# Splitting the first weight loads of a fused transformer block into transfers of 32 partitions

## The chip, the cores and the metric

The kernel runs on one core of one Trainium2 chip. The metric is the device time of one execution in microseconds (us), as the median of several runs. A core has a matrix engine (PE; its weight loads are listed apart, as PEld), a vector engine (DVE), a scalar engine (ACT), a general engine (POOL) and a synchronising engine (SP), and 16 DMA engines that they share. In this kernel SP does nothing but issue transfers: it walks through a list written by hand, waits at each entry for a semaphore, and issues.

## The reference

One layer of a hybrid block over 256 tokens of width 1024, all in float32:

```python
u = rmsnorm(h, norm_mix[i])
proj = u @ w_in[i]
y_rw  = rwkv7_mix(token_shift(proj[..., :RW_COLS], shift_mu[i]), ...)   # 8 heads x 64
y_gla = gla_mix(proj[..., RW_COLS:], ...)                               # 4 heads, 64 / 128
h = h + jnp.concatenate([y_rw, y_gla], axis=-1) @ w_out[i]
u = rmsnorm(h, norm_ffn[i])
h = h + moe(u, ...)        # top 4 of 32 experts; per expert w1 1024 x 2048, w2 1024 x 1024
u = rmsnorm(h, norm_ple[i])
h = h + jax.nn.sigmoid(u @ w_ple_gate[i]) * (p[i] @ w_ple[i])
return rmsnorm(h, norm_final)
```

The weights of all 32 experts are read, whatever the router picks: 8.39 MB of w1 and 4.19 MB of w2 for each expert, some 403 MB in all.

## The kernel before

**Stages.** The mixer comes first: norm, input projection, the RWKV heads by chunks of 64 tokens, the GLA heads, the output projection with `w_out`. Then the router, then the experts one after the other, then the gate of the per-layer embedding and the last norm. With the largest expert's token count at 64 or below, as here, each expert is one pass over 64 token slots: gather the tokens by a matmul, the w1 stage (`w1_stage`, line 1854), clamp and activation, the w2 stage (`w2_stage`, line 1882), and a scatter by a matmul into sums that stay open in PSUM.

**Weight buffers.** Every expert weight chunk is 128 partitions of 4096 floats, 16 KB in a partition, 2.097 MB in all. A w1 is four chunks, a w2 is two. There are four w1 buffers for even experts (`W1B[0]`, in the tensor `ring`), four for odd experts (`W1B[1]`, laid over the mixer's tensors `lg`, `ka`, `bu`, `bkv`), and two w2 buffers that all experts share (`W2B`, in `ring`). So even experts' buffers and w2 buffers come free as the mixer is done with that part of the ring, odd experts' buffers as the mixer is done with those tensors.

**First fill.** SP's list (lines 353 to 383) issues `w_out` in two loads of 2.097 MB (`load_wout`), and then the first fill of the ten expert buffers, ten loads of 2.097 MB, each behind its own wait: w1 of expert 0 in the order 0, 1, 3, 2 of its chunks, w1 of expert 1 in the order 0, 3, 1, 2, and both chunks of expert 0's w2. Between them stand a second load of `x` (1.05 MB, line 365) and the load of `b1` (line 375), 32 rows of 8 KB into 32 partitions.

**Stream.** Then SP waits for the router's count (`cnt_ok`, line 414) and runs `stream` (line 385): for each expert it waits until PE has used a chunk (`w1_used`, `w2_used`) and issues the load of the chunk that follows in that buffer. After the last w2 it issues the 4.19 MB of `w_ple_gate` into the ring (line 421), which the tail needs. All these loads are on SP's one queue, which each DMA engine works off in order. ACT issues two loads on a queue of its own when the first tokens are gathered (lines 758 and 759: `p` 0.26 MB, `w_ple` 1.05 MB).

**PE's waits.** A transfer adds 16 to its semaphore when it is complete. PE waits for `b1` at line 1800, for `w_out` at lines 1722 and 1761. In the w1 stage it waits for chunk 1 first (`start=START`), and then for each chunk as it comes to it:

```python
pe.wait_ge(on[start], h * 16 + 16)
for k in range(KC):
    if k % 2 == 0:
        pe.wait_ge(on[k // 2], h * 16 + 16)
```

Of the kernel before, what the change touches and what calls it, by code (L numbers as in the profile page):

```python
# [25 lines left out]
P = 128  # L26
# [49 lines left out]
def hybrid_block(nc, x, p, norm_mix, w_in, shift_mu, rw_w0, rw_w2, rw_a0, rw_a2, rw_g2, rw_kk, rw_ka, rw_rk,  # L76
# [8 lines left out]
    with ExitStack() as ctx:  # L85
# [9 lines left out]
        def slot(i, n=1):  # L95
            return RING[:, i * SLOT_F:(i + n) * SLOT_F]
# [65 lines left out]
            return a.rearrange("p (h t) -> p h t", h=HP)  # L162

        HALF = (slice(0, 64), slice(64, 128))


        MT = slot(2, 2).rearrange("p (m w) -> p m w", m=16)
# [38 lines left out]
        W1B = ([slot(2 * c, 2) for c in range(W1C)], [LG[:, 0:4096], KA[:, :], BU[:, :], BKV[:, :]])  # L206
        W2B = [slot(8 + 2 * c, 2) for c in range(W2C)]
# [18 lines left out]
        def col(name, i, n=1):  # L226
# [3 lines left out]
        x_in, x1_in, vec_in, small_in, wout_in, wout2_in, rows_in, brow_in, out_done = (  # L230
            sem(s) for s in ("x_in", "x1_in", "vec_in", "small_in", "wout_in", "wout2_in", "rows_in", "brow_in", "out_done"))
        nm_in, lora_in = sem("nm_in"), sem("lora_in")
        win = [sem(f"win{i}") for i in range(7)]
        landed_e = [sem(f"landed_e{i}") for i in range(W1C)]
        landed_o = [sem(f"landed_o{i}") for i in range(W1C)]
        landed_2 = [sem(f"landed_2{i}") for i in range(W2C)]
# [62 lines left out]
        w1_v = w1.rearrange("a e (c q j) n -> a e c q (j n)", q=P, j=2)  # L299
        w2_v = w2.rearrange("a e (c q j) n -> a e c q (j n)", q=P, j=4)  # L300
# [5 lines left out]
        def _(sp):  # L306
# [3 lines left out]
            def load_cols(i, s, n, c0, w):  # L310
                dst = RING[:, s * SLOT_F:s * SLOT_F + KC * w].rearrange("p (k n) -> p k n", k=KC)
                sp.dma_start(dst, w_in[0, :, c0:c0 + w].rearrange("(k q) n -> q k n", q=P)).then_inc(win[i], 16)

            def load_w1(e, odd, c):
                sp.dma_start(W1B[odd][c], w1_v[0, e, c]).then_inc((landed_o if odd else landed_e)[c], 16)

            def load_w2(e, c):
                sp.dma_start(W2B[c], w2_v[0, e, c]).then_inc(landed_2[c], 16)  # L318

            load_cols(0, 0, 1, 3 * RW, 256)  # L320
            for name, k in VROWS[1:]:
                sp.dma_start(VEC[VAT[name]:VAT[name] + k, :], vec_src[name]).then_inc(vec_in, 16)
# [23 lines left out]

            def load_wout(first, s, signal):

                sp.dma_start(slot(s, 2).rearrange("p (k n) -> p k n", k=4),
                             w_out[0, first:first + 512, :].rearrange("(k q) n -> q k n", q=P)).then_inc(signal, 16)  # L350

            sp.wait_ge(tile_ps, 18)
            sp.dma_start(GLN, gla_norm[0].partition_broadcast(P)).then_inc(rows_in, 16)
# [4 lines left out]
            for r, src in enumerate((rw_gn_w, rw_gn_b)):  # L358
                sp.dma_start(GNWB[:, r, :], src[0].partition_broadcast(P)).then_inc(rows_in, 16)
            sp.wait_ge(gg_ps, 2)  # L360
            load_w1(0, 0, 0)
            sp.wait_ge(go_ps, 2)
            load_w2(0, 0)
            sp.wait_ge(wu_ps, 2)
            sp.dma_start(XB3, x.rearrange("a (t q) d -> q (a t) d", q=P)).then_inc(x_in, 16)
            sp.wait_ge(y_gla, 1)
            load_w1(1, 1, 0)
            sp.wait_ge(reff_ps, 1)
            load_w1(0, 0, 1)
            sp.wait_ge(bv_ok, 1)  # L370
            load_w1(1, 1, 3)
            sp.wait_ge(o_ps, 3)
            load_w2(0, 1)
            sp.wait_ge(ovar, 3)
            sp.dma_start(B1R[0:NE, :], b1[0]).then_inc(b1_in, 16)
            sp.wait_ge(wg_used, 1)
            load_w1(0, 0, 3)
            sp.wait_ge(yt_ps, 4)
            load_w1(1, 1, 1)
            sp.wait_ge(wout_used, 1)  # L380
            load_w1(0, 0, 2)
            sp.wait_ge(lg_ps, 3)
            load_w1(1, 1, 2)

            def stream(nb):

# [852 lines left out]
        def _(pe):  # L1239
# [110 lines left out]
            for grp in TOK_ORDER:  # L1350
# [12 lines left out]
                if grp == 7:  # L1363
                    for first in range(2):
                        for h in range(HP):
                            for c in range(2):
                                for q in range(2):
                                    j, tt = (q, q) if first == 0 else (1 - q, q)
                                    rj = HALF[j]
                                    ins = mm(bank(6 + tt)[rj, P * h + 64 * c:P * h + 64 * (c + 1)],  # L1370
# [23 lines left out]
            def mats(n, u):  # L1394
# [5 lines left out]
                if n >= 2:  # L1400
                    pe.wait_ge(mat_ok, n - 1)
                quarters = [(c, j, HALF[j], slice(P * t + 64 * c, P * t + 64 * (c + 1)), slice(64 * c, 64 * (c + 1)))
                            for c in range(2) for j in range(2)]
# [315 lines left out]
            pe.wait_ge(h_ok, 3)  # L1719
            read_out()  # L1720
            pe.wait_ge(yt_a, 2)
            pe.wait_ge(wout_in, 16)
            w_out_gla(0, (4,))
            pe.wait_ge(reff_ok, 2)
            pe.wait_ge(o_ps, 2)
# [32 lines left out]

            ms = RT8[3]
            pe.wait_ge(yt_a, 3)  # L1760
            pe.wait_ge(wout2_in, 16)
            w_out_rest(0, 0, range(4))
            turn_rwkv(1)
            w_out_rest(0, 1, range(4)).then_inc(wout_ps, 1)
# [89 lines left out]
            def w1_stage(i, h, odd, start=START, ple=None):  # L1854

                pe.wait_ge(xg_ok, i + 1)
                pe.wait_ge(t_ok, i * 2 + 1)

                on = landed_o if odd else landed_e
                pe.wait_ge(on[start], h * 16 + 16)  # L1860
                for k in range(KC):
                    if k % 2 == 0:
                        pe.wait_ge(on[k // 2], h * 16 + 16)
                    w = W1B[odd][k // 2][:, 2048 * (k % 2):2048 * (k % 2 + 1)]
                    for half in range(2):
                        if ple is not None and k == 0 and half == 1:
                            pe.wait_ge(pt_ok, 2 * ple + 2)
                        mm(bank(4 + half)[0:64, :], XG[:, k, :], w[:, 512 * half:512 * (half + 1)], k == 0, k == KC - 1, True)
                        ins = mm(bank(4 + half)[64:128, :], XG[:, k, :], w[:, FF + 512 * half:FF + 512 * (half + 1)], k == 0, k == KC - 1, True)
                        if k == KC - 1 and half == 0:  # L1870
                            ins.then_inc(h0_ps, 1)
                    if k % 2:
                        ins.then_inc(w1_used, 1)
# [8 lines left out]
            def w2_stage(i, h, odd, last=False, ple=None, held=0):  # L1882

                if last:
                    turn_back(i, 6)
                else:
                    pe.wait_ge(oh_ok, i + 2)
                    if held:
                        pe.wait_ge(pt_ok, held)
                    gather()  # L1890
                pe.wait_ge(hs0, i + 1)
                for c in range(KC):
                    if c == 4:
                        pe.wait_ge(hs1, i + 1)
                    ins = pe.transpose(bank(4 + c // 4)[:, P * (c % 4):P * (c % 4 + 1)], HS[:, P * c:P * (c + 1)], ID[:, :])  # L1895
                    if c % 4 == 3:
                        ins.then_inc(t_ps, 1)
                pe.wait_ge(ys_ok, i + 1)
                scatter(scattered)
                for k in range(KC):  # L1900
                    if k == 4 and not last:
                        pe.wait_ge(t_ok, i * 2 + 3)
                        turn_back(i, 4)
                        gather_turn(i + 1)
                        if ple == 0:
                            pe.wait_ge(ple_in, 32)
                            for n in range(2):
                                for t in range(TT):
                                    ins = pe.transpose(bank(5)[:, 256 * n + P * t:256 * n + P * (t + 1)], PX[:, t, P * n:P * (n + 1)], ID[:, :])
                            ins.then_inc(pt_ps, 1)  # L1910
                    if k % 4 == 0:
                        pe.wait_ge(act_ok, i * 2 + (k // 4 + 1))
                        pe.wait_ge(landed_2[k // 4], h * 32 + 16 * (odd + 1))
                    w = W2B[k // 4][:, 1024 * (k % 4):1024 * (k % 4 + 1)]
                    mm(bank(7)[0:64, :], ACTT[:, k, :], w[:, 0:512], k == 0, k == KC - 1, True)
                    ins = mm(bank(7)[64:128, :], ACTT[:, k, :], w[:, 512:1024], k == 0, k == KC - 1, True)
                    if k % 4 == 3:
                        ins.then_inc(w2_used, 1)
                pe.wait_ge(ohgt_ok, i + 2)
                if ple is not None:  # L1920
                    pe.wait_ge(pt_ok, 1)
                    ple_product(1, ple)
                    pe.wait_ge(xg_ok, i + 2)
                    ple_product(0, ple)
# [34 lines left out]
            def tail():  # L1959

                def raised(t):

                    for g in range(2):
                        pe.wait_ge(scaled, 4 + 2 * t + g)
                        turned(t, range(4 * g, 4 * g + 4), g if t else 4 + g)

                raised(0)
                pe.wait_ge(wout_in, 32)
                for n, (t, c, w, b) in enumerate(UNITS):
                    if n == 1:  # L1970
                        raised(1)
                    for k in range(KC):
                        if k % 4 == 0:
                            pe.wait_ge(ut_v, 12 + 2 * t + k // 4)
                        ins = mm(bank(b)[:, 0:w], UT3[:, k, P * t:P * (t + 1)], PLG[:, k, c:c + w], k == 0, k == KC - 1)
                    ins.then_inc(pg_ps, 1)
# [33 lines left out]
```

## Time and profile before

| | before |
|---|---|
| median of 3 runs | 1161.89 us (1159.8 to 1163.87) |
| the profiled execution, its own time | 1160.67 us |
| span of its trace, first to last instruction | 1159.0 us |
| PE busy | 1097.5 us, 95% of the span |
| PE weight loads busy | 492.2 us, 42% |
| DVE, ACT, POOL busy | 317.4, 217.5, 54.5 us |
| DMA, mean over the span | 373 GB/s, 432.21 MB |
| granted clock of PE, mean | 0.984 |
| chain that ended last, by engine | PE 56%, DMA 40% |

The span is 1.7 us shorter than the execution's time. Busy time of PE counts matmuls from start to modelled end, pipelined ones too, so 95% doesn't say that PE is the bound. The chain that ended last is followed back from the last instruction: a DMA in it is a transfer that something waited for, from its issue to its landing, so the time in which it stood in its queue is in it.

### The profile page before, as it was taken

Reading aid. Unit: us, or ns where it says so; the run is one execution under the profiler, and the core shown is the slowest. Engines: PE = TensorE matmul, PEld = TensorE weight load, DVE = VectorE, ACT = ScalarE, POOL = GpSimd, SP = SyncE. Lnnn points to the kernel's source line nnn. Section 1 sums busy time; section 2 is a strip of 40 time slices with the busy share of each in tenths; the row PEclk is TensorE's granted clock in tenths of the full one; section 3 lists DMA queues with packets and bytes.
Section 4 is the critical chain, followed back from the end, with each engine's and each line's share of the span. In section 5 each row is a group of like instructions: output and inputs, shape, how many; then the busy total and the mean of one; then the engine's idle time right before and its main releaser. Section 6 shows DMA issues by size and latency. Waiting matters only on the chain.

```text
span 1159.0 us, 16059 instructions
## 1 busy us (share of the span) xinstructions
PE 1097.5 (95%) x6367; PEld 492.2 (42%) x6368; DVE 317.4 (27%) x736; ACT 217.5 (19%) x397; POOL 54.5 (5%) x104
## 2 busy tenths in 40 slices
PE   8999889999999999999999999999999999999997
PEld 6876774433333333333333333333333333333334
DVE  3363454322222222222222222222222222222223
ACT  3233222211112111111111111112111111111124
POOL 8005220000000000000000000000000000000000
PEclk9999999899999999999999999999999999999999
DMA  9621178899999999999999999999999999999970
GB/s 335 206 82 52 52 286 343 357 427 426 431 428 429 429 428 429 428 429 428 428 429 429 428 429 428 430 427 429 430 429 428 429 428 428 429 428 428 428 317 38
DMA packets 42095, 432.21 MB, mean 373 GB/s; under 512 B 5364, under 2 KB 8808, under 8 KB 16936
## 3 DMA queue, kind: packets, MB, share of 16 engines
q1 hardware_dynamic: 41352, 430.10, 88.7%
q10 hardware_dynamic: 704, 1.58, 0.4%
q8 instruction: 26, 0.43, 0.2%
q14 instruction: 13, 0.11, 0.0%
HBM read 430.62 MB, written 1.05 MB: 372 GB/s over the span
## 4 chain that ended last, share of the span: by engine, by line
PE 56%; DMA 40%; issue 1%; POOL 1%; DVE 1%; ACT 1%; SPq 0%; DVEq 0%; POOLq 0%; ACTq 0%
PE ps L1241 52%; DMA ring<-in_w_dram 37%; DMA ring<-in_w_ple_gate_dram 2%; PE ps L1895 1%; PE ps L1822 1%; PE ps L1879 0%; DMA xb<-in_x_dram 0%; POOL xb L533 0%; PE ps L1743 0%; PE ps L1530 0%; ACT bu L662 0%; PE ps L1797 0%; SPq L318 0%; PE ps L1377 0%; POOL ring L518 0%
## 5 line engine op out<-in xcount | busy, mean ns | idle before, releaser
L1241 PE MATMUL ps<-ring,ay 128*64 128x512 f32 x1024 | 242.1, 616 | 37.2 <-DMA ring<-in_w_dram 36.2
L1241 PE MATMUL ps<-ring,gqk 128*64 128x512 f32 x1024 | 224.1, 595 | 2.8 <-DMA ring<-in_w_dram 2.6
L1156 DVE COPY t<-ps 128x512 f32<-128x512 f32 x32 | 22.1, 692 | 491.7 <-PE ps L1241 491.7
L1241 PEld LDWEIGHTS ps<-ring,ay 128*64 128x64 f32 x1024 | 72.5, 140 | 182.1 <-issue 132.6
L1241 PEld LDWEIGHTS ps<-ring,gqk 128*64 128x64 f32 x1024 | 79.0, 138 | 144.8 <-issue 140.2
L1241 PE MATMUL ps<-ring,bu 128*128 128x512 f32 (+1 forms) x240 | 88.2, 514 | 0.5 <-DMA ring<-in_w_ple_gate_dram 0.5
L766 ACT ACTIVATE t<-ps 128x512 f32<-128x512 f32 x32 | 19.1, 597 | 358.7 <-PE ps L1241 358.7
L1241 PE MATMUL ps<-bu,ring 128*128 128x256 f32 (+2 forms) x352 | 66.5, 354 | 1.2 <-DVE bu L840 1.2
L1241 PE MATMUL ps<-yb,ohgt 64*128 64x512 f32 x264 | 65.6, 615 | 0.8 <-ACT yb L781 0.8
L1241 PE MATMUL ps<-xb,oh 128*64 128x512 f32 x256 | 62.5, 607 | 0.0
L1241 PEld LDWEIGHTS ps<-bu,ring 128*128 128x128 f32 (+1 forms) x352 | 57.5, 182 | 9.9 <-DMA ring<-in_w_in_dram 1.4
L1241 PE MATMUL ps<-lg,gqk 128*64 128x512 f32 x256 | 57.9, 593 | 0.7 <-DMA ka<-in_w_dram 0.7
L1161 DVE TENSOR_TENSOR t<-ps,gqk 128x512 f32<-128x512 f32 x64 | 44.0, 687 | 53.4 <-PE ps L1895 53.3
L1241 PEld LDWEIGHTS ps<-ring,bu 128*128 128x128 f32 x240 | 43.8, 190 | 34.1 <-issue 30.5
L1241 PE MATMUL ps<-bkv,gqk 128*64 128x512 f32 x256 | 57.8, 592 | 0.0
L1241 PE MATMUL ps<-bu,gqk 128*64 128x512 f32 x256 | 57.8, 592 | 0.0
L1241 PE MATMUL ps<-ka,gqk 128*64 128x512 f32 x256 | 57.8, 592 | 0.0
L1122 DVE TENSOR_TENSOR gqk<-ps,vc 128x512 f32<-128x512 f32 x32 | 22.1, 692 | 122.8 <-PE ps L1822 122.8
L773 ACT ACTIVATE t<-ay 128x256 f32<-128x256 f32 x64 | 26.6, 416 | 90.3 <-DVE ay L1166 90.3
L781 ACT ACTIVATE yb<-ps 128x512 f32<-128x512 f32 x32 | 19.1, 597 | 125.3 <-PE ps L1241 125.3
L1895 PEld LDWEIGHTS ps<-id,t 128*128 128x128 f32 x256 | 27.4, 141 | 25.4 <-issue 25.1
L764 ACT ACT_TABLE_LOAD x28 | 35.9, 1283 | 2.5 <-issue 2.0
(359 smaller groups left out, 807.3 us busy)
## 6 DMA issues: line engine op xcount, KB each, us to landing
ring<-in_w_dram SPq DMA_DIRECT2D x128, 2048.0 KB, 24.6
lg<-in_w_dram SPq DMA_DIRECT2D x16, 2048.0 KB, 26.0
bkv<-in_w_dram SPq DMA_DIRECT2D x16, 2048.0 KB, 31.3
ka<-in_w_dram SPq DMA_DIRECT2D x16, 2048.0 KB, 28.2
bu<-in_w_dram SPq DMA_DIRECT2D x16, 2048.0 KB, 29.2
ring<-in_w_in_dram SPq DMA_DIRECT2D x5, 2048.0 KB, 20.1
ring<-in_w_out_dram SPq DMA_DIRECT2D x2, 2048.0 KB, 8.7
ring<-in_w_ple_gate_dram SPq DMA_DIRECT2D x1, 4096.0 KB, 28.1
```

What stands on the lines that cost most here:

```text
L764: act.activation(SM[:, 126:127], SM[:, 100:101], ACT.Sigmoid)
L766: act.activation(HS[:, 0:512].rearrange("p (j q) -> p j q", j=4), bank(4).rearrange("p (q j) -> p j q", j=4), ACT.Copy).then_inc(hs0, 1)
L773: act.activation(SIG[:, 4 * g:4 * g + 4], GLU[:, 4 * g:4 * g + 4], ACT.Sigmoid, scale=1.702).then_inc(sig_ok, 1)
L781: act.activation(YS, bank(7), ACT.Copy).then_inc(ys_ok, 1)
L1122: dve.tensor_tensor(XG.rearrange("p (h q) s -> p q h s", h=2), bank(6).rearrange("p (q h s) -> p q h s", q=4, h=2), col("norm_ffn", 0, 8). ...
L1156: dve.tensor_copy(HS[:, 512:1024].rearrange("p (j q) -> p j q", j=4), bank(5).rearrange("p (q j) -> p j q", j=4)).then_inc(hs1, 1)
L1161: dve.tensor_tensor(TP[:, cs].rearrange("p c (g s) -> p c g s", g=2), bank(4 + g).rearrange("p (c g s) -> p c g s", c=4, g=2), B1T[:, bass ...
L1241: return pe.matmul(out_, lhs, rhs, start=start, stop=stop, skip_group_check=shared)
L1822: ins = pe.transpose(bank(6)[:, P * q:P * (q + 1)], paired(XGR, q), ID[:, :])
L1895: ins = pe.transpose(bank(4 + c // 4)[:, P * (c % 4):P * (c % 4 + 1)], HS[:, P * c:P * (c + 1)], ID[:, :])
```

## The change

`w_out` and the first fill of the ten expert buffers, twelve loads of 128 partitions, are issued as four transfers of 32 partitions each, one behind the other on SP's queue. Each transfer adds 16 to the same semaphore as before, so PE waits for 64 where it waited for 16, and in the stream, whose loads stay whole, for 48 more than before. Nothing else moves: every wait of SP, the order of the loads and their bytes are the same.

```diff
+        QUARTERS = tuple(slice(32 * i, 32 * i + 32) for i in range(4))
...
+            def first_w1(e, c):
+                for q in QUARTERS:
+                    sp.dma_start(W1B[e][c][q, :], w1_v[0, e, c][q, :]).then_inc((landed_o if e else landed_e)[c], 16)
+
+            def first_w2(c):
+                for q in QUARTERS:
+                    sp.dma_start(W2B[c][q, :], w2_v[0, 0, c][q, :]).then_inc(landed_2[c], 16)
...
             def load_wout(first, s, signal):
 
-                sp.dma_start(slot(s, 2).rearrange("p (k n) -> p k n", k=4),
-                             w_out[0, first:first + 512, :].rearrange("(k q) n -> q k n", q=P)).then_inc(signal, 16)
+                for q in QUARTERS:
+                    sp.dma_start(slot(s, 2).rearrange("p (k n) -> p k n", k=4)[q],
+                                 w_out[0, first:first + 512, :].rearrange("(k q) n -> q k n", q=P)[q]).then_inc(signal, 16)
...
             sp.wait_ge(gg_ps, 2)
-            load_w1(0, 0, 0)
+            first_w1(0, 0)
             sp.wait_ge(go_ps, 2)
-            load_w2(0, 0)
+            first_w2(0)
...
-            pe.wait_ge(wout_in, 16)
+            pe.wait_ge(wout_in, 64)
...
-                pe.wait_ge(on[start], h * 16 + 16)
+                pe.wait_ge(on[start], h * 16 + 64)
                 for k in range(KC):
                     if k % 2 == 0:
-                        pe.wait_ge(on[k // 2], h * 16 + 16)
+                        pe.wait_ge(on[k // 2], h * 16 + 64)
...
-                        pe.wait_ge(landed_2[k // 4], h * 32 + 16 * (odd + 1))
+                        pe.wait_ge(landed_2[k // 4], h * 32 + 16 * odd + 64)
...
-                pe.wait_ge(wout_in, 32)
+                pe.wait_ge(wout_in, 80)
```

## Rows read from the trace of the kernel before

**Rows 1.** Page, part 2: DMA busy tenths and rate, 40 slices of 29 us.

```profile
DMA  9621178899999999999999999999999999999970
GB/s 335 206 82 52 52 286 343 357 427 426 431 428 429 429 428 429 428 429 428 428 429 429 428 429 428 430 427 429 430 429 428 429 428 428 429 428 428 428 317 38
```

**Rows 2.** Chain that ended last, 960 to 1160 us: start, us, what.

```profile
1095.31 28.06 DMA ring<-in_w_ple_gate_dram
1123.37 0.04 issue
1123.41 7.13 PE ps L1241 x16
```

**Rows 3.** Stretch of the stream: busy time by engine, PE clock, DMA share, GB/s.

```profile
369.00:1118.00 749.00, 708.95 (x3308) 268.18 (x3306) 166.57 (x418) 111.56 (x205) 0.00 (x0) 0.99 1.01 428
```

**Rows 4.** Chain that ended last, 225 to 400 us.

```profile
237.06 0.48 PE ps L1822 x4
...
263.61 0.47 PE ps L1822 x4
...
369.62 24.25 DMA ring<-in_w_dram
```

**Rows 5.** SP's issues in order: start us, us until the last was issued.

```profile
77.40 33.48 SPq L349 DMA_DIRECT2D ring<-in_w_out_dram  x2
...
142.92 0.33 SPq L315 DMA_DIRECT2D ring<-in_w_dram  x1
149.64 0.33 SPq L318 DMA_DIRECT2D ring<-in_w_dram  x1
...
177.37 0.33 SPq L375 DMA_DIRECT2D t<-in_b_dram  x1
185.18 0.33 SPq L315 DMA_DIRECT2D ring<-in_w_dram  x1
...
203.74 0.33 SPq L315 DMA_DIRECT2D bu<-in_w_dram  x1
218.23 10.57 SPq L315 DMA_DIRECT2D ring<-in_w_dram  x4
236.88 4.75 SPq L318 DMA_DIRECT2D ring<-in_w_dram  x2
```

**Rows 6.** Stretches of the first fill, columns as in rows 3.

```profile
142.00:145.00 3.00, 2.75 (x22) 1.88 (x24) 1.04 (x2) 1.38 (x3) 0.00 (x0) 1.00 0.47 93
143.00:219.20 76.20, 71.08 (x835) 45.28 (x836) 34.61 (x83) 21.21 (x42) 7.59 (x6) 0.93 0.81 311
...
164.50:171.00 6.50, 6.50 (x172) 5.28 (x166) 3.69 (x8) 0.00 (x0) 0.00 (x0) 1.00 0.19 45
...
219.20:223.00 3.80, 3.80 (x22) 1.49 (x20) 0.60 (x2) 0.20 (x1) 0.00 (x0) 1.00 1.04 361
```

**Rows 7.** Stretches around transfers that fill only part of the partitions, columns as in rows 3.

```profile
172.00:186.00 14.00, 14.00 (x59) 6.71 (x51) 9.04 (x16) 2.27 (x5) 0.00 (x0) 1.00 0.99 421
186.00:190.00 4.00, 4.00 (x14) 1.94 (x13) 0.42 (x1) 0.38 (x1) 0.00 (x0) 1.00 1.03 289
8.25:10.75 2.50, 1.18 (x6) 0.89 (x7) 1.42 (x5) 0.38 (x1) 2.09 (x7) 1.00 1.09 204
5.00:8.00 3.00, 2.21 (x18) 1.82 (x16) 1.61 (x4) 1.06 (x4) 2.73 (x5) 1.00 1.08 367
```

**Rows 8.** SP's four loads of one w1 with nothing to wait for.

```profile
976.52 2.24 SPq L315 DMA_DIRECT2D ring<-in_w_dram  x4
```

**Rows 9.** PE in order: output projection, transposes of b1, first w1 stage.

```profile
169.31 1.98 PE L1241 MATMUL ps<-ring,bu 128*128 128x512 f32 x4
...
204.41 1.14 PE L1797 MATMUL ps<-id,t 32*128 32x32 f32 x8
...
214.34 13.95 PE L1241 MATMUL ps<-ring,gqk 128*64 128x512 f32 x64 [0.23 <-DVE gqk L1122]
```

**Rows 10.** DMA issues by line: count, KB of one, median us from issue to landing.

```profile
ring<-in_w_out_dram SPq DMA_DIRECT2D x2, 2048.0 KB, 8.7
```

**Rows 11.** POOL in order, behind the second w_out load.

```profile
119.66 2.35 POOL L542 TENSOR_TENSOR ka<-ka,bu 128x1024 f32<-128x1024 f32 x1 [2.55 <-DMA bu<-in_rw_gn_b_dram]
128.80 1.27 POOL L546 TENSOR_TENSOR lg<-lg,ka 128x512 f32<-128x512 f32 x1 [6.79 <-ACT ka L685]
```

More of the change, by code:

```diff
@@ L366, in _ @@
             sp.wait_ge(y_gla, 1)
-            load_w1(1, 1, 0)
+            first_w1(1, 0)
             sp.wait_ge(reff_ps, 1)
-            load_w1(0, 0, 1)
+            first_w1(0, 1)
             sp.wait_ge(bv_ok, 1)
-            load_w1(1, 1, 3)
+            first_w1(1, 3)
             sp.wait_ge(o_ps, 3)
-            load_w2(0, 1)
+            first_w2(1)
             sp.wait_ge(ovar, 3)
@@ L376, in _ @@
             sp.wait_ge(wg_used, 1)
-            load_w1(0, 0, 3)
+            first_w1(0, 3)
             sp.wait_ge(yt_ps, 4)
-            load_w1(1, 1, 1)
+            first_w1(1, 1)
             sp.wait_ge(wout_used, 1)
-            load_w1(0, 0, 2)
+            first_w1(0, 2)
             sp.wait_ge(lg_ps, 3)
-            load_w1(1, 1, 2)
+            first_w1(1, 2)
             def stream(nb):
@@ L1760, in _ @@
             pe.wait_ge(yt_a, 3)
-            pe.wait_ge(wout2_in, 16)
+            pe.wait_ge(wout2_in, 64)
             w_out_rest(0, 0, range(4))
```

## The prediction, made before the changed kernel ran

> **What bounds the kernel now.** I read the page's slices first [rows 1]: from the ninth slice, 232 us, to 1101 us the DMA engines are busy in every slice and move 426 to 431 GB/s, and that traffic ends within the last slice but one. PE's 95% is no contradiction, since its busy time is modelled from pipelined matmuls. The chain says what ended it [rows 2]: the tail's first gate matmul at 1123.41 waits for `w_ple_gate`, the last load of SP's queue, issued at 1095.31 behind all others. The windows confirm it: over 749 us of the stream the DMA share is 1.01 at 428 GB/s [rows 3]. An expert is 12.58 MB, 29.4 us at that rate, while PE, when nothing makes it wait, takes 263.61 - 237.06 = 26.55 us [rows 4]. So the DMA queue is the bound from the stream's first load to `w_ple_gate`, PE eats up its head start of two experts until it first waits at 369.62 [rows 4], and the end moves with one thing alone: **when the first load of the stream gets its turn on the queue.** That was 219.2, one us behind its issue at 218.23 [rows 5].
>
> Before that, the queue has slack. The first fill runs from 143.6 (142 to 145 is busy for 0.47 of 3 us, issue at 142.92) to 219.2, and from 143.0 on 311 GB/s x 76.2 us = 23.70 MB were moved [rows 6]: ten chunks of 2.097 MB, 20.97 MB, and 2.73 MB of other loads. At 428 GB/s that is 55.4 us. Some 20 us were not used, in stretches where SP waits for a buffer to come free; 164.5 to 171 is one, at 45 GB/s [rows 6].
>
> **The change part by part.** *Bytes and gates:* the same loads at the same waits. Nothing can start sooner, and a chunk counts as landed only with its fourth transfer.
>
> *Issues.* Twelve loads become 48. With nothing to wait for, four issues take SP 2.24 us [rows 8], so each load costs it 1.9 us more than the 0.33 us of one. The first of four transfers occupies the engines for over 1.2 us even at 428 GB/s, longer than the 0.58 us to the next issue, so no engine runs dry. The three loads that come closest (169.4 to 172.5) would have SP busy to about 176.4, before the wait that ends at 177.37 [rows 5]. I cost it at nothing; uncovered it would be 12 x 1.9 = 23 us of SP, of which only what lies ahead of an empty queue counts.
>
> *Rate of a 32-partition transfer.* This carries everything. The trace has two places where transfers fill only part of the partitions. The 0.26 MB of `b1`, 32 partitions, issued at 177.37 behind three chunks, are moved in 186 to 190: the rate falls from 421 to 289 GB/s, with the engines as busy as before (0.99 and 1.03) [rows 7]. The two loads of 64 partitions each at 8.25 to 10.75 run at 204 GB/s and share 1.09, against 367 just before [rows 7]. So such a transfer does not use fewer engines; it makes each packet last longer. The bounds: at best it runs like a whole chunk, 428 GB/s and 4.9 us for 2.097 MB. It can't gain, since the engines are at share 1.01 already. At worst it costs what `b1` cost with its edges: 4 x (421 - 289) = 528 KB not moved, 1.25 us, and its own 0.62 us, so 1.87 us for 262 KB, 140 GB/s and 15.0 us for a chunk. I take about half rate, the 204 GB/s of the row nearest to a continuous run, and 214, half of 428: 209 GB/s, **10.0 us for a chunk**. The loss at `b1` above half rate I put down to the change-over between two kinds of transfers, which a run of forty alike has only at its ends.
>
> The Trainium skill has a rule against this change: by "SBUF — State Buffer", section "Door 1: The DMA port swizzle", a range of 32 partitions reaches 8 of the 16 ports through which DMA writes, with an asymptote of 218 GB/s and 189 GB/s measured at 1 MiB. The direction agrees with the 204 and 289 GB/s of [rows 7]; by its two figures a chunk would take 9.6 or 11.1 us and the estimate would be 1187 or 1202 us.
>
> *The sum.* With chunks of 10.0 us the queue never runs dry: the second chunk is issued at 149.64, before the first ends at 153.6, and so on. The other 2.73 MB at some 400 GB/s are 6.8 us. The stream's first load starts at 143.6 + 100 + 6.8 = 250.4 instead of 219.2: 31.2 us later. The rate of 361 in 219.2 to 223, where the second chunk wasn't released yet [rows 6], becomes 428: (428 - 361) x 3.8 us = 255 KB, 0.6 us back. So +30.6 us on the profiled execution's 1160.67 us (its span of 1159.0 and 1.7 us around it): **1191 us**. That execution is 1.2 us below the median of the runs, so on the median it would be 1192.5.
>
> *Does PE keep the queue filled?* `b1` lands behind six chunks at 143.6 + 60 + 4 + 1 = 208.6, and PE wants it at 204.41 [rows 9]: 4 us late. The first w1 stage starts at 218.5, reaches chunk 2 after half its 13.95 us [rows 9], at 225.5, and waits for the ninth load, 143.6 + 90 + 6.8 + 1 = 241.4. The stage ends at 248.4 instead of 228.3, 20 us late. That costs nothing by itself: the queue is 31 us late. Its first four stream loads are released by 248.4, and the w2 loads, issued 8.6 and 13.3 us behind the stage's end before (236.88, 4.75 us for two [rows 5]), by 262, while the queue has work until 250.4 + 4 x 4.9 = 270. From there PE is 11 us nearer to the queue than it was, so it first waits about 11 / 2.85 = 4 experts sooner, near 290.
>
> *Output weight.* Two loads, 5 us longer each. The first, at 77.40, is needed at 169.31 [rows 5, 9]. The second ends near 123; behind it stand two row loads for which POOL already waits until 119.66. It would start at 124.5 and end at 127, before the wait that ends at 128.80 [rows 11]. Hidden, with 2 us to spare; were it not, POOL's work up to line 552 would move by what is over.
>
> **The rivals.**
>
> *The slack swallows it (not slower).* The price of the change is paid only once the ten chunks together fill the 219.2 - 143.6 - 6.8 = 68.8 us that they have: the point is 6.9 us for a chunk, 305 GB/s. If 32-partition transfers in a row reach that, for instance because engines that have drifted apart write to different places, the stream starts at 219.2 as before: 1161 us, no change, or a hair less where PE's first wait shifts. For it: it is 20 us, and no trace shows a long run of such transfers. Against it: both rows of part transfers lie below 305 at full share [rows 7].
>
> *Each transfer has a price of its own.* At `b1` 1.87 us were paid where half rate asks 1.25; if the other 0.62 us belong to every transfer and not to the change-over, a chunk pays it four times: 12.5 us, start at 275.4, +55.6 us, 1216 us. For it: the same excess at 8.25 us, where (367 - 204) x 2.5 = 408 KB were lost on 262 KB. Against it: in the stream loads follow each other at 428 GB/s with nothing between them [rows 3], four times as large though. The Trainium skill, "DMA: Bandwidth & Descriptors", section "Anatomy of one DMA", has a fixed price of some 2 us for a transfer, given for GpSimd's path; four of them on top of 10 us would be an estimate of 1271 us, and [rows 3] has no sign of it between loads in one queue.
>
> *PE takes over.* If the late first experts left PE behind the queue, the stream would starve. It would need PE to be more than 31 us late where I find 20, at which point each further us is one of the result. 1195 to 1200 us.
>
> **How the numbers follow.** Half rate 0.72, its own range 1182 to 1204 (chunks of 9.1 to 11.3 us). Own price for each transfer 0.13. A rate between half and 305 GB/s, 1165 to 1182: 0.05. PE takes over 0.02. The slack swallows it 0.08, of which 0.02 come out faster by over 0.3%. A measurement of this kernel can tell 0.3%, 3.5 us, from no change. So slower 0.92, same 0.06, faster 0.02. The range reaches down to chunks of 8.5 us (1176) and up to 12.7 us (1218): it takes in most of the second rival and leaves out the bound of 15.0 us (1241) and the slack.
>
> **What would show it.** Right: `w_out` lands some 14 us after its issue instead of 8.7 [rows 10]; slices from 143 to 250 us run near 210 GB/s with a DMA share near 1; SP still issues the stream's first load near 222, but its data move from 250; PE waits for `ring` in the first w1 stage for some 16 us; the stream keeps 428 GB/s and the wait for `w_ple_gate` ends near 1154. Wrong: `w_out` lands as before, or the stream starts at 219 all the same; then the time is that of before. If the rate of the slices is 140 to 170, the second rival is right.

## The result

The changed kernel takes 1200.95 us (median of 4 runs, 1200.74 to 1203.42), the kernel before 1161.25 us in the same comparison. The ratio is 1.0344, 95% interval 1.0321 to 1.0368: 40 us slower where 30.6 were forecast, and inside the range. The profiled execution took 1201.0 us, its span is 1199.3 us.

The page's slices of the changed kernel, DMA busy tenths and rate, to be read against [rows 1]:

```profile
DMA  9532298999999999999999999999999999999970
GB/s 338 185 79 61 58 219 187 213 292 428 428 428 428 428 428 428 428 428 428 428 428 428 428 428 428 428 428 428 428 429 428 428 428 429 428 428 427 427 328 36
```

The slices are 30 us now. From the tenth on, up to the last two, nothing has changed: 427 to 429 GB/s. In the sixth to eighth, where the first fill is, the rate fell from 286, 343 and 357 GB/s to 219, 187 and 213, with the engines as busy or busier. The chain that ended last still goes through the last load of the queue, as in [rows 2]:

```profile
1135.91 27.79 DMA ring<-in_w_ple_gate_dram
1163.70 0.06 issue
1163.76 7.12 PE ps L1251 x16
```

The tail's first gate matmul starts at 1163.76 instead of 1123.41, 40.35 us later; behind it nothing moved. The windows of the changed kernel, columns as in [rows 3] (us, busy time of five engines, PE clock, DMA share, GB/s), say where these 40 us were lost:

```profile
146.80:259.00 112.20, 84.22 (x876) 50.78 (x877) 35.52 (x86) 21.47 (x43) 7.59 (x6) 0.86 0.97 210
183.90:259.00 75.10, 59.22 (x281) 28.08 (x282) 21.57 (x63) 12.86 (x27) 0.00 (x0) 0.86 1.01 215
179.20:182.60 3.40, 2.51 (x79) 2.24 (x76) 1.70 (x4) 0.00 (x0) 0.00 (x0) 1.00 0.14 34
182.60:183.90 1.30, 0.93 (x12) 0.62 (x12) 0.43 (x1) 0.00 (x0) 0.00 (x0) 1.00 0.00 0
259.00:1158.00 899.00, 854.04 (x3974) 321.38 (x3970) 202.71 (x509) 135.43 (x248) 0.00 (x0) 0.98 1.01 428
```

The first fill takes from 146.8 to 259 us, at 210 GB/s in the mean, where it took from 143.6 to 219.2 [rows 6]. While it is continuous (183.9 to 259) it runs at 215 GB/s with the engines at share 1.01: half rate, as forecast. The stream behind it is the old one. But the third and fourth rows are a hole in the queue, 4.7 us long, that the forecast did not have, and the fill began 3.2 us late. SP's issues show why, against [rows 5]:

```profile
77.37 34.81 SPq L359 DMA_DIRECT2D ring<-in_w_out_dram  x8
...
146.12 1.73 SPq L323 DMA_DIRECT2D ring<-in_w_dram  x4
152.85 1.70 SPq L327 DMA_DIRECT2D ring<-in_w_dram  x4
...
183.39 2.75 SPq L323 DMA_DIRECT2D ring<-in_w_dram  x4
...
217.72 1.71 SPq L323 DMA_DIRECT2D bu<-in_w_dram  x4
232.19 27.33 SPq L316 DMA_DIRECT2D ring<-in_w_dram  x4
```

Every gate of the fill is late: the first by 3.2 us (146.12 against 142.92), the fourth chunk's by 14.0 (183.39 against 169.4), the last by 14.0 (217.72 against 203.74). SP itself was idle at these waits; the mixer on PE was late. PE's timeline has the places, each the instruction behind a stretch of idle time (in brackets; "issue" is time in which the profile shows nothing that it waited for). First the kernel before, then the changed one:

```profile
121.42 0.37 PE L1241 MATMUL ps<-xb,bu 64*64 64x64 f32 x2 [2.17 <-issue]
157.77 1.21 PE L1241 MATMUL ps<-bkv,ring 64*128 64x128 f32 x16 [2.03 <-issue]
```

```profile
124.39 0.37 PE L1251 MATMUL ps<-xb,bu 64*64 64x64 f32 x2 [5.18 <-issue]
158.67 3.63 PE L1251 MATMUL ps<-ay,bu 64*64 64x128 f32 x64 [3.97 <-issue]
168.75 2.08 PE L1251 MATMUL ps<-bkv,ring 64*128 64x128 f32 x16 [5.50 <-issue]
177.63 0.27 PE L1251 MATMUL ps<-bkv,ring 64*64 64x64 f32 x1 [1.11 <-issue]
182.97 0.39 PE L1251 MATMUL ps<-ring 64*64 64x64 f32 x10 [1.26 <-issue]
```

Before, PE lost 4.2 us in two such holes; now 17.0 us in five, 12.8 us more. What was on the DMA engines just then is in the DMA view of short windows: queue, packets, MB, share of the engines. The kernel before at 118.5 to 120.5 us, then the changed kernel at 121 to 123:

```profile
q1 hardware_dynamic: 70, 0.11, 14.6%
q8 instruction: 1, 0.02, 2.9%
```

```profile
q1 hardware_dynamic: 240, 0.48, 96.1%
q8 instruction: 1, 0.02, 4.0%
```

One packet of instructions, 16 KB, ran there; the view counts it on the same 16 DMA engines as the weights (q1). In the changed kernel there is none from 118.5 to 120.5; it comes near the end of the second `w_out` load, and PE goes on about 1.5 us behind it. The hole at 163 us is alike: an instruction packet in 165.6 to 167.6, PE goes on at 168.75. The trace has such a packet for each of the seven holes, before and after, and PE goes on 1.4 to 1.7 us behind its end.

The places of the holes say that it is PE's code. In the columns of the windows, PE and PEld count PE's instructions. These are the stretches of the changed kernel from its second hole to the third, from the third to the fourth and from the fourth to the fifth:

```profile
158.60:163.30 4.70, 4.57 (x128) 4.43 (x127) 1.65 (x3) 1.19 (x2) 0.06 (x1) 0.64 1.05 220
168.60:176.60 8.00, 7.78 (x127) 7.31 (x127) 2.99 (x6) 1.09 (x2) 0.00 (x0) 0.76 1.09 261
177.60:181.80 4.20, 4.08 (x127) 3.81 (x128) 1.70 (x4) 0.00 (x0) 0.00 (x0) 1.00 0.51 109
```

That is 255, 254 and 255 instructions. From the first hole to the second it is 1524, six times 254, with six packets; in the kernel before it is 1779 between its two holes, seven times 254, with seven packets. So these holes stand only where a block of 254 or 255 instructions is used up, at the same places of both programs, and a packet comes for each block.

So the theory is: *half rate fills the queue past its slack, as forecast, and besides, code loads of PE stand behind the slow transfers, make PE idle in the mixer, whose many small matmuls use up code fast, and so delay SP's gates.*

### The profile page after: what moved, and what is told of

It reads as the page before. It is cut to its first block, busy times and chain, and to the rows that moved or that the text cites. A ratio compares the mean times of both kernels' runs of the same rounds, so it can differ in the third digit from the quotient of the medians.

```text
span 1199.3 us, 16095 instructions
## 1 busy us (share of the span) xinstructions
PE 1108.0 (92%) x6367; PEld 497.0 (41%) x6368; DVE 317.0 (26%) x736; ACT 217.4 (18%) x397; POOL 54.4 (5%) x104
## 4 chain that ended last, share of the span: by engine, by line
PE 50%; DMA 45%; issue 2%; POOL 1%; ACT 1%; DVE 1%; SPq 0%; POOLq 0%; DVEq 0%; ACTq 0%
PE ps L1251 47%; DMA ring<-in_w_dram 43%; DMA ring<-in_w_ple_gate_dram 2%; PE ps L1905 1%; PE ps L1832 0%; DMA xb<-in_x_dram 0%; PE ps L1889 0%; ACT bu L672 0%; POOL xb L543 0%; PE ps L1540 0%; PE ps L1753 0%; SPq L319 0%; PE ps L1387 0%; POOL ring L528 0%; DVE ay L925 0%
## 5 line engine op out<-in xcount | busy, mean ns | idle before, releaser
L1251 PE MATMUL ps<-ring,ay 128*64 128x512 f32 x1024 | 247.2, 627 | 41.6 <-DMA ring<-in_w_dram 40.8
L1251 PE MATMUL ps<-ring,gqk 128*64 128x512 f32 x1024 | 227.1, 601 | 17.0 <-DMA ring<-in_w_dram 16.7
L786 ACT ACTIVATE ohgt<-ps 128x256 f32<-128x256 f32 x32 | 12.3, 383 | 134.4 <-PE ps L1889 134.4
```

The source lines that it names most:

```text
L786: act.activation(OHGT[:, :], bank(6 if last else 4)[:, 0:T], ACT.Copy).then_inc(ohgt_ok, 1)
L1251: return pe.matmul(out_, lhs, rhs, start=start, stop=stop, skip_group_check=shared)
```

## The experiments

The rivals: that the price belongs to each transfer and not to its range of partitions; and that the 10 us beyond the forecast are slower chunks, gates playing no part. All ratios are to the kernel before, with 95% intervals.

**Four transfers, all partitions.**

```diff
-        QUARTERS = tuple(slice(32 * i, 32 * i + 32) for i in range(4))
+        QUARTERS = tuple(slice(1024 * i, 1024 * i + 1024) for i in range(4))
...
-                    sp.dma_start(W1B[e][c][q, :], w1_v[0, e, c][q, :])...
+                    sp.dma_start(W1B[e][c][:, q], w1_v[0, e, c][:, q])...
```

> The same twelve loads in four transfers each, but each transfer over all 128 partitions, a quarter of the columns (4 KB of a row). If the range of partitions of a transfer sets its rate, the chunks take 4.9 us as before and the time is 1161 us, within 4 us. If each transfer has a price of its own (the chunk's 9.8 us being 4.9 us and four times 1.2 us), the time is that of the changed kernel, 1201 us.

1162.36 us, ratio 1.0015 (1.0004 to 1.0026). Same number of transfers, bytes and semaphore counts, and nearly none of the 40 us. The time alone would not settle it, since the slack hides anything up to 6.9 us for a chunk; the rate does. The window of this kernel that answers to 172 to 186 in [rows 7], and a stretch in which its queue is full:

```profile
172.00:186.00 14.00, 14.00 (x82) 6.95 (x81) 9.04 (x16) 2.27 (x5) 0.00 (x0) 1.00 0.94 333
182.00:188.00 6.00, 6.00 (x19) 2.84 (x18) 1.33 (x2) 0.60 (x1) 0.00 (x0) 1.00 1.03 418
```

The 333 GB/s are not the rate of such transfers: the share is 0.94, as SP took 3.13 and 4.35 us for the four issues of two chunks there, where 1.75 us is usual in this run, and the first 4 us run at 211 to 248 GB/s. From 176 to 182 it is 336 to 360, why stays open; behind that, with the queue full, it is 418 GB/s, 5.0 us for a chunk. So transfers of a quarter of the columns run at the rate of whole chunks, those of a quarter of the partitions at half of it: the range of partitions is what costs.

**Two transfers of 64 partitions.**

```diff
-        QUARTERS = tuple(slice(32 * i, 32 * i + 32) for i in range(4))
+        QUARTERS = tuple(slice(64 * i, 64 * i + 64) for i in range(2))
```

> The same twelve loads in two transfers of 64 partitions each. If the rate goes by the ports that a range of partitions reaches, and 0 to 63 reaches no more than 0 to 31, a chunk still takes 9.8 us and the time is 1195 to 1205 us. If it is a price for each transfer, a chunk takes 4.9 + 2 x 1.2 = 7.4 us, the fill ends near 224 to 230 and the time is 1165 to 1172 us; the same if the rate grew with the number of partitions.

1202.3 us, 1.0359 (1.0338 to 1.038): twice the partitions, half the transfers, and the same time as with 32. The continuous part of the fill:

```profile
185.00:220.00 35.00, 33.83 (x177) 17.31 (x175) 16.20 (x37) 7.86 (x19) 0.00 (x0) 1.00 1.00 211
```

211 GB/s, and the holes are the same (5.14, 4.20, 4.90, 1.07, 0.99 us). The rate does not grow with the number of partitions between 32 and 64. This is what the Trainium skill, "SBUF — State Buffer", section "Door 1: The DMA port swizzle", says: 0 to 63 reaches the same 8 ports as 0 to 31, asymptote 218 GB/s; the traces agree with 211 to 215.

**Eight transfers of 16 partitions.** The same line with `16` and `range(8)`. As with the halves, PE's waits for the semaphores follow the number of transfers.

> The same twelve loads in eight transfers of 16 partitions each. If the rate goes by the range of partitions, 16 partitions have half the rate of 32, some 105 GB/s and 19.6 us for a chunk: ten of them end near 350, 130 us behind the 219 of before, and with later gates the time is 1285 to 1330 us. If it is a price for each transfer, a chunk takes 4.9 + 8 x 1.2 = 14.5 us and the time is 1235 to 1260 us. If any part transfer runs at half rate, whatever its range, the time is 1201 us.

1274.97 us, 1.0985 (1.0959 to 1.1011): slower than the price for each transfer allows and faster than the range theory said.

```profile
213.00:240.00 27.00, 27.00 (x79) 13.04 (x77) 12.03 (x20) 5.22 (x12) 0.00 (x0) 1.00 1.00 120
210.00:290.00 80.00, 49.72 (x246) 25.25 (x244) 20.18 (x59) 12.27 (x26) 0.00 (x0) 0.80 1.01 125
255.00:310.00 55.00, 16.79 (x76) 8.75 (x76) 4.59 (x21) 3.50 (x5) 0.00 (x0) 0.62 1.01 132
```

The last two stretches have the load of `b1` and ACT's loads in them, the first has these transfers alone. The rate falls again, to 120 GB/s, but not to the 105 that I had put by halving once more. By the same section of the Trainium skill 16 partitions reach 4 ports, asymptote some 109 GB/s: here the measurement is above it. Why was not tried. Nor was a transfer of 64 partitions taken from both halves of the 128, which would tell the range of partitions from their number.

**Only the output weight split.**

```diff
-            first_w1(0, 0)
+            load_w1(0, 0, 0)
...
-                pe.wait_ge(on[start], h * 16 + 64)
+                pe.wait_ge(on[start], h * 16 + 16)
```

and the same for the other nine chunks.

> Only the two output weight loads in transfers of 32 partitions, the ten first fill loads whole. If PE's idle time near 119 us, which has no waited-for work in the trace, is a load of its code that stands behind the second output weight load on the same DMA engines, that idle time is 5.2 us as in the changed kernel instead of 2.2, all gates of the fill come 3 us late and the time is 1164 us. If the output weight has nothing to do with it, the idle time is 2.2 us and the time is 1161 us.

1163.8 us, 1.0029 (1.0013 to 1.0045), and PE's holes:

```profile
124.01 0.37 PE L1251 MATMUL ps<-xb,bu 64*64 64x64 f32 x2 [4.87 <-issue]
160.68 1.16 PE L1251 MATMUL ps<-bkv,ring 64*128 64x128 f32 x16 [2.02 <-issue]
```

The first hole has grown to 4.87 us, the second is as before, and the first gate is at 145.84 instead of 142.92. No engine waits for these loads' data any longer than before, but they cost 3 us.

**Only the first three chunks, only the last seven, only the last four.** The same edit, with those chunks left in four transfers and `w_out` whole.

> Only the first three chunks (issued at 142.9, 149.6 and 156.6 us) in four transfers of 32 partitions, the output weight and the other seven whole. Their 15 us of extra transfer time fit into idle time of the queue before 219 us. If late loads of PE's code are what slows the mixer, PE has idle time of 4 and 5.5 us near 155 and 163 us, all later gates come 8 to 10 us late, the stream with them, and the time is 1169 to 1172 us. If transfer time alone counts, it is hidden, and the time is 1161 us; if every chunk has its share, 1173 us.

1173.29 us, 1.0110 (1.0093 to 1.0127). The transfer time of these chunks fits into the queue's idle time; the run shows it, since the queue runs empty again just ahead of the stream:

```profile
225.00:230.00 5.00, 4.77 (x23) 2.50 (x24) 0.74 (x2) 0.90 (x3) 0.00 (x0) 0.90 0.36 92
```

What it costs are holes of 3.94, 5.23, 0.81 and 2.08 us in PE, and gates that are 12.7 us late at the stream (230.93 against 218.23). This is the second term by itself. The time is above the 1169 to 1172 us expected and is also what equal shares would give; the gates and the empty queue tell the two apart.

> The output weight and the first three chunks of the fill whole, the other seven chunks in four transfers of 32 partitions. These seven are issued from 169.4 us on, behind the mixer's small matmuls. If the part of the slowdown beyond the forecast comes from late loads of PE's code in the mixer, the mixer now runs as before, the gates come as before, and the fill ends at 171 + 7 x 9.8 + 4.4 = 244 us instead of 219.2: 1183 to 1187 us. If instead every chunk has its share of the 40 us, 7/10 of it is 28 us: 1189 us. If the chunks themselves take 10.8 us and gates play no part: 251 us, 1191 us.

1186.94 us, 1.0227 (1.0211 to 1.0242). PE's holes in the mixer are those of before (2.12 and 1.94 us, and one of 0.49), the gates come as before, and the fill still ends near 244 us: the first term by itself, as put by the sum. Slower chunks with no part for the gates would have given 1191 us, equal shares 1189.

> Only the last four chunks in four transfers of 32 partitions. By the queue's account they run from 187.5 us to 227 us, with the two loads of ACT beside them the fill ends near 230 us instead of 219.2, and the time is 1169 to 1172 us. If every chunk has its share of the 40 us, it is 1177 us; if the slack swallows four chunks' 20 us, it is 1161 us.

1173.35 us, 1.0108 (1.0093 to 1.0124), against 1169 to 1172 put by the queue's account and 1177 by equal shares: between them, nearer the account. Gates are as before. `w_ple_gate`, issued at 1108.51 and landed 27.7 us later, was there just as the PE chain of the last experts ended, and the tail's gate matmul started at 1136.35, 12.9 us later than before, where the account has 10.8. Why the end came 2 us later still is open.

The three parts without overlap, output weight, first three and last seven, add up to 0.29 + 1.10 + 2.27 = 3.66% beside 3.44% (3.21 to 3.68) for the whole. About 2.3% are transfer time past the slack, 1.2 to 1.4% late gates. The queue's end says the same: with the seven alone it is near 244, 24.8 us behind the 219.2 of before, and gates that are 14.0 us late make it 38.8 of the 39.8 measured.

**Loads moved out of the way of the code.** If a code load stands behind a weight load, moving the weight load in the kernel before should close a hole. The second `w_out` load, whole, goes behind the third chunk:

```diff
-            sp.wait_ge(gla_el, 3)
-            load_wout(0, 4, wout2_in)
             sp.wait_ge(mat_ps, 8)
...
             load_w1(1, 1, 0)
+            sp.wait_ge(gla_el, 3)
+            load_wout(0, 4, wout2_in)
```

> The kernel before with one change: the second output weight load, whole, is issued behind the fill's third chunk (near 157 us, a stretch in which the queue runs empty) instead of at 110.5 us. If PE's idle time of 2.2 us near 119 us is a code load that stands behind this load, it is gone, SP's gates up to 157 us come 2 us sooner, and the time is 1158 to 1161 us, depending on whether the code loads near 163 us then stand behind it. If that idle time has nothing to do with this load, it stays at 2.2 us.

1161.46 us, 1.0003 (0.9994 to 1.0012). The hole at 119 us is gone, and the third chunk is issued at 153.43 instead of 156.59. The fourth comes at 169.14, hardly sooner than 169.44: the second hole has grown from 2.03 to 2.50 us, one of 0.80 us behind it is new, and PE ran longer at its lower clock, as the rows at the end of this section show.

The next run issues it at 168 us, ahead of the fourth chunk (the line behind `sp.wait_ge(reff_ps, 1)`).

> The kernel before with the second output weight load, whole, issued at 169 us ahead of the fill's fourth chunk instead of at 110.5 us. If code loads that stand behind weight loads are what makes PE idle in the mixer, the idle time near 119 us is gone as in the run that moved it to 154 us, and now no weight load is in the way of the code loads near 163 to 166 us: all gates come 2 to 3 us sooner, the stream too, and the time is 1157 to 1159 us. If the queue's order counts and not the code, the fill's later chunks are 4.9 us later and the time is 1161 us or more.

1159.89 us, 0.9987 (0.9977 to 0.9997): half of what was expected. The hole at 119 is 0.47 us, the one at 155 is now 2.62.

The last one moves the second chunk behind the third as well. Its diff, beside the two lines taken out above:

> As the run before it, and the fill's second chunk (w2, at 149.6 us) is issued behind the third. If PE's idle time of 2.0 us near 156 us is a code load behind that chunk, it is gone or smaller, and the time is 1155 to 1158 us. If the third chunk then stands in the way of the code load near 161 us instead, nothing is won against the run before it.

```diff
-            sp.wait_ge(go_ps, 2)
-            load_w2(0, 0)
             sp.wait_ge(wu_ps, 2)
...
             load_w1(1, 1, 0)
+            sp.wait_ge(go_ps, 2)
+            load_w2(0, 0)
             sp.wait_ge(gla_el, 3)
             sp.wait_ge(reff_ps, 1)
+            load_wout(0, 4, wout2_in)
```

1156.34 us, 0.9961 (0.9947 to 0.9975), faster than both kernels. PE's holes in its mixer:

```profile
119.53 0.27 PE L1241 MATMUL ps<-xb,bu 64*64 64x64 f32 x2 [0.25 <-issue]
...
149.00 1.98 PE L1241 MATMUL ps<-ay,bu 64*64 64x128 f32 x64 [0.19 <-issue]
164.21 0.39 PE L1241 MATMUL ps<-ring 64*64 64x64 f32 x10 [1.25 <-issue]
```

With one of 0.21 us between them, 1.9 us are left of 4.2, and the stream is issued at 213.66 instead of 218.23, 4.57 us sooner. Nothing but the order of whole loads was changed, so the holes hang on which weight load is in the queue. That the late thing is PE's code is read from the instruction packets, from the places of the holes and from these moves; PE's own fetch was not seen waiting.

The gain is larger than the holes that were closed, and PE's granted clock (third column from the end) goes with the rest. The same window of the kernel before, the changed one, the one with `w_out` moved and the last:

```profile
150.00:172.00 22.00, 18.86 (x442) 16.07 (x442) 12.18 (x21) 4.69 (x10) 4.06 (x4) 0.92 0.70 260
150.00:172.00 22.00, 12.53 (x286) 11.32 (x283) 8.82 (x15) 4.97 (x10) 7.18 (x6) 0.78 1.01 226
150.00:172.00 22.00, 17.66 (x394) 15.32 (x387) 10.22 (x19) 1.84 (x4) 2.25 (x2) 0.84 0.85 324
150.00:172.00 22.00, 19.84 (x426) 15.27 (x419) 14.63 (x27) 3.78 (x8) 2.54 (x2) 1.00 0.89 346
```

Where the mean is below 1, PE ran part of the window at the lower of its two levels, 1.2 instead of 2.4 GHz: from 160 to 162, behind a hole, the granted clock is 0.50 both before and after. The 64 matmuls behind the changed kernel's second hole take 3.63 us there, where the same 64 take 1.98 us in the last kernel. So gates can be 14.0 us late for holes that have grown by 12.8, and closing 2.3 us of holes could give 4.57 us.

## Why the prediction was right, and by how much not

*The bound.* Right: the queue's end sets the time, 428 GB/s from the fill's end to 1158, the wait for `w_ple_gate` near 1154 in the forecast, at 1163.70 in the run.

*The rate.* Right: 209 GB/s assumed, 215 measured in the continuous part, and 211 for halves. The rival of a price for each transfer is refuted by four transfers over all partitions (418 GB/s with the queue full, ratio 1.0015) and by halves that cost what quarters do. That the excess at `b1` belongs to the change-over is not shown; it only isn't paid by each transfer.

*The slack.* Right in kind: the transfer time of three slow chunks alone was hidden, the queue ran empty again behind them, and seven alone end near the 244 us of the sum. A chunk between 5 and 6.9 us was not tried.

*Gates.* Wrong, and this is the term that was left out: "the same loads at the same waits" took for granted that the waits would end when they did. SP's waits hang on PE's mixer, PE's mixer hangs on its code, and its code comes through the DMA engines that I was slowing down. SP issued the stream's first load at 232.19, not near 222. Fill's end forecast 250.4, measured 259.0: 3.2 us of late start, 4.7 us in which the queue ran dry (179.2 to 183.9, where I had written that it never does), and 0.7 us that I did not break down. That 1201 us lies inside the range of half rate too, 1182 to 1204, is in part luck: that range was for chunks of up to 11.3 us, and they ran at the forecast rate.

*Output weight.* "Hidden" was half wrong. Its data are not waited for any longer, and POOL's wait ends at 125.23 where I had 124.5, without cost [rows 11]. But it delays the code load at 119 us by 3 us, the whole kernel with it.

*PE and the queue.* Right in kind: PE waits 14.15 us for chunk 2 in its first w1 stage (16 forecast), the queue stays filled, and PE first waits in the stream at 320.70, earlier than at 369.62 [rows 4] though not as early as the 290 put.

## What to carry to other kernels

Look up which partitions a transfer covers before you split it: split the free dimension and keep all 128 partitions, since ranges of 32 or 64 ran at half the rate here. When a queue has slack, work out for how many microseconds it lasts; below that point a slower load costs nothing, above it every microsecond is one of the result. And read "issue" holes of PE against the DMA view: where small matmuls use up code fast, a large load in the queue at the wrong moment cost PE 2 to 5 us here, and more where the granted clock fell behind it. Moving that load cost no transfer time.

## What the hardware showed that was not expected

PE's code loads run on the DMA engines that also move the data, and with a large load in the queue they come late: in the kernel before this cost 4.2 us in two holes, in the changed one 17.0, with 16 partitions up to 10.3 us for a single hole. The Trainium skill, "Runtime: NRT & Kernel Launch", section "Instruction fetch mechanics", has the blocks of 16 KiB that an engine's sequencer fetches on a queue of its own and calls the cost mostly hidden; the traces agree with the size (26 packets of the changed kernel are 0.43 MB) and not with "hidden" at these holes.
